# x and the query columns first, decode keys, values and S5 inputs in a later unit: a hybrid decoder step on one core

## The reference, cut to what matters

```
hn = rmsnorm(x, ln1_g)                     # x: 1024 prompt rows + 8 decode rows, width 1024
q, k, v, u = split(hn @ w_in)              # four groups of 512 columns
q, k = rope_partial(q) / 8, rope_partial(k)
attn = subln(softmax(q1 k1) v - lam * softmax(q2 k2) v)     # 4 heads, two maps each
                                           # prompt: causal; decode: 64 cache pages + the new key
s5   = glu(gelu(scan of 32 complex diagonal states driven by u))
x = x + concat(attn, s5) @ w_out
x = x + hierarchical_moe(rmsnorm(x))       # 32 experts, two per token
y = rmsnorm(x)                             # outputs also: new k, v and S5 states
```

## Time and profile before

| | us |
|---|---|
| median of 3 runs | 1478.14 (1476.67 to 1494.74) |
| profiled execution | 1475.24 |
| its span | 1473.5 |
| TensorE busy | 1284.7 (87%) |
| VectorE busy | 522.2 (35%) |
| ScalarE busy | 248.1 (17%) |
| POOL busy | 212.9 (14%) |
| mean of DMA | 311 GB/s |

### The profile page before, as it was taken

The page is one execution under the profiler, slowest core; times in us unless marked ns, Lnnn a source line. Parts: engine busy times, 40 slices in busy tenths (PEclk is TensorE's granted clock), DMA queues, the critical chain, the costliest instruction groups (busy, mean ns, idle before and its releaser), DMA issues.

```text
span 1473.5 us, 26489 instructions
## 1 busy us (share of the span) xinstructions
PE 1284.7 (87%) x8952; PEld 670.8 (46%) x8952; DVE 522.2 (35%) x1430; ACT 248.1 (17%) x473; POOL 212.9 (14%) x327
## 2 busy tenths in 40 slices
PE   4799899999889878899869999987799999999930
PEld 2455565654334335566654443433344444444410
DVE  1461344443564555455531121134221121112126
ACT  2200111120122222233321000000111111111111
POOL 1101204040401100000010000000112222222121
PEclk9899999999988989999999999986999999999975
DMA  9499979979987987999996998998899999999754
GB/s 355 173 318 317 340 258 304 344 236 319 313 286 250 366 285 251 368 330 312 325 372 253 337 337 294 314 348 309 284 332 363 368 372 360 367 364 373 259 202 186
DMA packets 186454, 458.35 MB, mean 311 GB/s; under 512 B 24177, under 2 KB 24561, under 8 KB 177778
## 3 DMA queue, kind: packets, MB, share of 16 engines
q1 hardware_dynamic: 165906, 394.41, 75.6%
q0 software_dynamic: 20448, 62.59, 12.7%
HBM read 421.92 MB, written 33.80 MB: 309 GB/s over the span
## 4 chain that ended last, share of the span: by engine, by line
PE 71%; DMA 9%; DVE 8%; SPq 5%; issue 3%; DVEq 2%; ACT 1%; POOL 1%; ACTq 0%; POOLq 0%; PEldq 0%
PE WA L1764 53%; PE SC L1764 7%; PE OD L1764 6%; DMA ring<-in_cacheK 3%; SPq L489 3%; DMA ring<-in_cacheV 2%; PE WA L2110 2%; DMA arena<-in_x_s 1%; SPq L477 1%; PE WA L1865 1%; DVE arena L1733 1%; DVE st L1105 1%; DMA ring<-h_scratch,idc 1%; DMA xm<-in_xT 1%; DVE arena L1746 1%
## 5 line engine op out<-in xcount | busy, mean ns | idle before, releaser
L1764 PE MATMUL WA<-arena 128*128 128x512 f32 (+9 forms) x1440 | 351.8, 428 | 15.3 <-issue 7.1
L1764 PE MATMUL WA<-arena,xm 128*128 128x512 f32 (+2 forms) x768 | 315.7, 619 | 8.7 <-DMA arena<-in_w_out 6.6
L1764 PEld LDWEIGHTS WA<-arena 128*128 128x128 f32 (+2 forms) x1440 | 192.6, 195 | 148.6 <-issue 132.6
L1764 PEld LDWEIGHTS WA<-arena,xm 128*128 128x128 f32 (+1 forms) x768 | 123.5, 182 | 164.1 <-issue 155.9
L1764 PE MATMUL WA<-xm,arena 128*128 128x512 f32 x192 | 88.8, 610 | 1.7 <-ACT arena L936 1.3
L553 POOL TENSOR_TENSOR st<-st,consts 128x1 f32<-128x1 f32 (+2 forms) x18 | 13.8, 765 | 465.5 <-DVEq L1139 279.0
L1764 PE MATMUL OD<-ring,sall 128*32 128x512 f32 x512 | 69.8, 660 | 11.9 <-DMA ring<-in_cacheV 11.9
L1764 PE MATMUL OD<-ring,qpad 128*32 128x128 f32 x2048 | 64.1, 275 | 8.9 <-DMA ring<-in_cacheK 8.7
L1764 PE MATMUL SC<-ring,qpad 128*32 128x128 f32 x2048 | 64.4, 276 | 7.7 <-DMA ring<-in_cacheK 7.5
L1676 DVE TENSOR_TENSOR xm<-WA,colw 128x960 f32<-128x960 f32 x16 | 18.5, 1158 | 147.1 <-PE WA L2110 147.1
L1676 DVE TENSOR_TENSOR arena<-WA,colw 128x960 f32<-128x960 f32 x16 | 18.5, 1158 | 137.5 <-PE WA L2110 137.3
(11 more groups left out here) (359 smaller groups left out, 1250.0 us busy)
## 6 DMA issues: line engine op xcount, KB each, us to landing
ring<-in_cacheK SPq DMA_DIRECT2D x512, 256.0 KB, 4.7
ring<-in_cacheV SPq DMA_DIRECT2D x512, 256.0 KB, 4.7
arena<-in_w_gu SPq DMA_DIRECT2D x16, 2048.0 KB, 8.6
arena<-in_w_dn SPq DMA_DIRECT2D x16, 1024.0 KB, 12.5
ring<-in_w_gu SPq DMA_DIRECT2D x8, 2048.0 KB, 8.6
xm<-in_w_gu SPq DMA_DIRECT2D x8, 2048.0 KB, 8.6
arena<-in_w_in SPq DMA_DIRECT2D x32, 256.0 KB, 10.2
ring<-in_w_dn SPq DMA_DIRECT2D x8, 1024.0 KB, 12.6
```

Source lines behind the costliest of these rows:

```text
L1764: return pe.matmul(out, lhsT, rhs, start=first, stop=last, **kw)
```

## The change

The loads of SP are issued in another order: all of x, then `w_q`, then `w_u`, then the pages. `w_k` and `w_v` come in two loads of 2 MB from POOL's queue, once `qpad` is written. POOL issues only three loads ahead of the statistics; the other six follow the root. `dqkv` is replaced by `dq` (queries alone, four column groups of 128 columns, ahead of the 9 one-column products) and by `dkv` and `dk2` (keys, values and u), planned later; `dprep` is a planned unit, carried out by VectorE ahead of its first `u` evacuation. `qpad` is written by 8 copies. The planner begins with other values of its bank, page and pace counters. `lam` moves behind the queries.

```diff
@@ -59,7 +59,8 @@
     return {
-"stats": [(("ss",), 2)], "dqkv": [(("dp",), 1)], "dprep": [(("rep",), 2), (("dqt",), 1)],
+"stats": [(("ss",), 2)], "dq": [(("dp",), 1)], "dprep": [(("dqt",), 1), (("rep",), 2)],
+"dkv": [(("dkv",), 1)], "dk2": [(("dkt",), 1)],
 "u": [(("u",) + a[:2], 1)] if first else [],
@@ -79,12 +80,12 @@
-    dec = []
+    dec = [(("dprep",), 2.5, [(("dq",), 6.0)])]
     for x in range(NPASS):
...
         for y in range(SPP):
-            dec.append((("K", x, t, g, y), 1.95, [(("ov", SPP * x - 1), 0.8)] if x else []))
+            dec.append((("K", x, t, g, y), 1.95, [(("ov", SPP * x - 1), 0.8)] if x else [(("dprep",), 0.5)]))
 dec += [(("m1", x), 0.8, [(dec[-1][0], 0.9)]), (("m2", x), 0.3, [(("m1", x), 3.3)]),
@@ -106,6 +107,9 @@
     proj += [(("u", n, a, f), half, []) for f in range(2)]
+    if (n, a) == (3, 0):
+        proj.append((("dkv",), 7.5, [(("dprep",), 20.0)]))
+    proj.append((("dk2",), 0.9, [(("dkv",), 6.0)]))
     for i in range(NT):
@@ -136,9 +140,9 @@
-    s5 = [(("s5a",), 0.0, [])]
+    s5 = [(("s5a",), 0.0, [(("dprep",), 2.0)])]
     for n in range(NQ):
-x = [(("bY", n - 1, 1), 0)] if n else [(("u", 3, 1, 1), 4.0), (("s5a",), 60.0)]
+x = [(("bY", n - 1, 1), 0)] if n else [(("u", 3, 1, 1), 4.0), (("dk2",), 3.0), (("s5a",), 60.0)]
@@ -178,9 +182,9 @@
     at = {k: 0 for k in lists}
-    end, free, nxt = {}, [0.0] * BANKS, 0
-    plan, t = [("stats",), ("dqkv",), ("dprep",)], 0.0
-    land, gone, due = [0.0, 0.0], [], 0.0
+    end, free, nxt = {("dq",): 0.0}, [0.0] * BANKS, 3
+    plan, t = [("stats",), ("dq",)], 0.0
+    land, gone, due = [4.0, 10.0], [], 4.0
     kept, never = {}, 1e9
@@ -258,6 +262,10 @@
+    first = PLAN.index(("u", 0, 0, 1))
+    DVE_PLAN = PLAN[:first] + [("dprep",)] + [u for u in PLAN[first:] if u != ("dprep",)]
+    assert PLAN.index(("dprep",)) > first
     POW = {}
...
@@ -473,8 +482,10 @@
         sp.dma_start(xm[:, k, :], io["xT"][k, :, :]).then_inc(s_xk[k], 16)
-        for n, w in enumerate((w_q, w_k, w_v, w_u)):
-            sp.dma_start(w[:, k, :], io["w_in"][n, k, :, :]).then_inc(s_wk[k], 16)
+    for k in range(KD):
+        sp.dma_start(w_q[:, k, :], io["w_in"][0, k, :, :]).then_inc(s_wq, 16)
+    for k in range(KD):
+        sp.dma_start(w_u[:, k, :], io["w_in"][3, k, :, :]).then_inc(s_wk[k], 16)
@@ -536,17 +547,16 @@
     gp.dma_start(rope[:, :, :], io["rope"]).then_inc(s_cst, 16)
-    gp.dma_start(br[:, :], io["b_r"].partition_broadcast(128)).then_inc(s_cst, 16)
-    gp.dma_start(wr[:, :, :], io["w_r"]).then_inc(s_cst, 16)
-    gp.dma_start(bglu[:, :], io["b_glu"]).then_inc(s_cst, 16)
-    gp.dma_start(lamv[:, :, :], io["lamv"].partition_broadcast(128)).then_inc(s_lamv, 16)
-    gp.dma_start(par, io["s5_par"]).then_inc(s_ld5, 16)
-    gp.dma_start(bc, io["s5_bc"]).then_inc(s_ld5, 16)
     def stats():
         gp.memset(qpad[:, :, :, :], 0.0).then_inc(s_qbd, 1)
-        gp.wait_ge(s_cst, 96)
+        gp.wait_ge(s_cst, 48)
         root(rstd[:, :], ("stats",))
+        gp.dma_start(lamv[:, :, :], io["lamv"].partition_broadcast(128)).then_inc(s_lamv, 16)
+        gp.dma_start(bglu[:, :], io["b_glu"]).then_inc(s_lamv, 16)
+        gp.dma_start(br[:, :], io["b_r"].partition_broadcast(128)).then_inc(s_lamv, 16)
+        gp.dma_start(wr[:, :, :], io["w_r"]).then_inc(s_lamv, 16)
+        gp.dma_start(par, io["s5_par"]).then_inc(s_ld5, 16)
+        gp.dma_start(bc, io["s5_bc"]).then_inc(s_ld5, 16)
@@ -559,17 +569,22 @@
-    def dqkv():
-        gp.wait_ge(s_drope, 1)
+    def dprep():
+        gp.wait_ge(s_qbd, 2)
+        for n, w in enumerate((w_k, w_v)):
+            gp.dma_start(w, io["w_in"][n + 1, :, :, :].rearrange("k p n -> p k n")).then_inc(s_wkv, 16)
+    def dkv():
+        gp.wait_ge(s_drope, 2)
         gp.dma_start(io["v_s"], dv[:, :]).then_inc(s_dst, 16)
...
-    def dprep():
-        gp.wait_ge(*filled("dqt"))
+    def dk2():
+        gp.wait_ge(*filled("dkt"))
         gp.memset(U[:, :, 0:NB], 0.0)
...
         gp.drain().then_inc(s_uz, 1)
-        gp.wait_ge(s_qbd, 2)
+        gp.wait_ge(s_qbd, 3)
...
@@ -732,10 +747,10 @@
-    def dqkv():
+    def dq():
         act.wait_ge(*filled("dp"))
-        for n, out in enumerate((qk[0:NB, 0:QKW], qk[0:NB, QKW:2 * QKW], dv[:, :], du)):
-            act.activation(out, slot("dp")[32 * n:32 * n + NB, 0:QKW], ACT.Copy)
+        for c in range(4):
+            act.activation(qk[0:NB, 128 * c:128 * c + 128], slot("dp")[32 * c:32 * c + NB, 0:128], ACT.Copy)
         act.drain().then_inc(free_sem("dp"), 1)
@@ -743,6 +758,15 @@
         act.drain().then_inc(free_sem("rep"), 1)
+        act.wait_ge(s_lam, 1)
+        act.activation(lamt[:, 2:4], lamt[:, 0:2], ACT.Exp).then_inc(s_lam, 1)
+    def dkv():
+        act.wait_ge(*filled("dkv"))
+        for n, out in enumerate((qk[0:NB, QKW:2 * QKW], dv[:, :], du)):
+            act.activation(out, slot("dkv")[32 * n:32 * n + NB, 0:QKW], ACT.Copy)
+        act.drain().then_inc(free_sem("dkv"), 1)
+        act.drain().then_inc(s_dq, 1)
@@ -752,7 +776,7 @@
         else:
-            act.wait_ge(*filled("dqt"))
+            act.wait_ge(*filled("dkt"))
             act.wait_ge(s_dst, 48)
@@ -916,9 +940,7 @@
-    act.wait_ge(s_lam, 1)
-    act.activation(lamt[:, 2:4], lamt[:, 0:2], ACT.Exp).then_inc(s_lam, 1)
...
@@ -1004,22 +1026,27 @@
     def lam():
-        dve.wait_ge(s_lamv, 16)
+        dve.wait_ge(s_lamv, 64)
         dve.tensor_tensor(lamv[:, 0, :], lamv[:, 0, :], lamv[:, 1, :], MUL)
...
         dve.drain().then_inc(s_lam, 1)
+    def lam_map():
         dve.wait_ge(s_lam, 2)
...
         dve.drain()
+        dve.scalar_tensor_tensor(wmap[:, 0:SPP, :].rearrange("p y h -> p (y h)"), consts[:, C_M1:C_M1 + SPP * H],
+                                 lamt[:, 7:8], consts[:, C_M0:C_M0 + SPP * H], MUL, ADD)
+        dve.drain()
...
     def stats():
-        lam()
-        dve.wait_ge(s_cst, 96)
+        dve.memset(rstd[:, NT:NT + 1], 1.0)
+        dve.wait_ge(s_cst, 48)
         for k in range(KD):
@@ -1028,46 +1055,55 @@
         dve.drain().then_inc(free_sem("ss"), 1)
-        dve.memset(rstd[:, NT:NT + 1], 1.0)
-        dve.scalar_tensor_tensor(wmap[:, 0:SPP, :].rearrange("p y h -> p (y h)"), consts[:, C_M1:C_M1 + SPP * H],
-                                 lamt[:, 7:8], consts[:, C_M0:C_M0 + SPP * H], MUL, ADD)
-        dve.drain()
         dve.wait_ge(s_col, 1)
...
         root(("stats",))
+        dve.drain().then_inc(s_rstd, 1)
+    def dq():
+        dve.wait_ge(s_dq, 1)
+        dve.tensor_scalar(qk[0:NB, 0:QKW], qk[0:NB, 0:QKW], rstd[0:NB, NT:NT + 1], None, MUL)
+        dve.drain()
+        rotate(qk[0:NB, 0:QKW], NB, NT)
+        dve.drain().then_inc(s_drope, 1)
+        for i in range(NT):
+            dve.tensor_scalar(diag[:, i, :], ident, rstd[:, i:i + 1], None, MUL)
+        dve.drain().then_inc(s_rep, 1)
+    def dprep():
+        dve.wait_ge(s_qbd, 1)
+        dve.wait_ge(*filled("dqt"))
+        src = slot("dqt")[:, 0:H * NB].rearrange("p (h x y) -> p h x y", h=H, y=SPP)
+        for h in range(H):
+            for c in range(2):
+                dve.tensor_copy(qpad[64 * c:64 * c + 64, h, :, :].rearrange("p (x y) n -> p x (y n)", y=SPP)
+                                [:, :, 2 * h + c::40], src[64 * c:64 * c + 64, h, :, :])
+        dve.drain().then_inc(free_sem("dqt"), 1)
+        dve.drain().then_inc(s_qbd, 1)
+        lam()
         dve.tensor_scalar(bglu[:, :], bglu[:, :], 0.5, None, MUL)
...
         dve.memset(st[:, :], 1.0)
...
-        dve.drain().then_inc(s_rstd, 1)
-        for i in range(NT):
-            dve.tensor_scalar(diag[:, i, :], ident, rstd[:, i:i + 1], None, MUL)
-        dve.drain().then_inc(s_rep, 1)
-    def dqkv():
-        dve.wait_ge(s_dq, 1)
+        dve.drain()
+    def dkv():
+        lam_map()
+        dve.wait_ge(s_dq, 2)
         r = rstd[0:NB, NT:NT + 1]
-        dve.tensor_scalar(qk[0:NB, :], qk[0:NB, :], r, None, MUL)
+        dve.tensor_scalar(qk[0:NB, QKW:2 * QKW], qk[0:NB, QKW:2 * QKW], r, None, MUL)
         dve.tensor_scalar(dv[:, :], dv[:, :], r, None, MUL)
...
         dve.drain()
-        rotate(qk[0:NB, :], NB, NT)
+        rotate(qk[0:NB, QKW:2 * QKW], NB, NT)
         dve.drain().then_inc(s_drope, 1)
...
-    def dprep():
-        dve.wait_ge(s_qbd, 1)
-        dve.wait_ge(*filled("dqt"))
-        src = slot("dqt")[:, 0:2 * H * NB].rearrange("p (a h b) -> p a h b", a=2, h=H)
-        for h in range(H):
-            for c in range(2):
-                for y in range(SPP):
-                    dve.tensor_copy(qpad[64 * c:64 * c + 64, h, y::SPP, 8 * y + 2 * h + c],
-                                    src[64 * c:64 * c + 64, 0, h, y::SPP])
-        dve.tensor_copy(knT[:, :, :], src[:, 1, :, :])
-        dve.tensor_copy(usT, slot("dqt")[:, 2 * H * NB:3 * H * NB].rearrange("p (n b) -> p n b", n=4))
-        dve.drain().then_inc(free_sem("dqt"), 1)
+    def dk2():
+        dve.wait_ge(*filled("dkt"))
+        dve.tensor_copy(knT[:, :, :], slot("dkt")[:, 0:H * NB].rearrange("p (h b) -> p h b", h=H))
```

(48 more changed lines are left out.)

13 lines of the change are left out of this document (7 added, 6 removed).

## The result

The changed kernel took 1464.5 us (median of 4 runs, 1460.34 to 1464.86), the kernel before 1479.36 beside it: ratio 0.9885, 95% interval 0.9851 to 0.9919. It is 15 to 17 us shorter, less than the 2% that count as a difference here. The forecast was 1461 within 1446 to 1475. The profiled execution took 1464.86, its span is 1463.1; before it was 1475.24 and 1473.5. The kernel before was profiled once only, so how far its own places move from one execution to the next is not known.

What follows compares the result with a forecast made beforehand. TensorE was taken as nearly always busy from 60.6 to 1050 us, the opening using neither TensorE nor DMA well. Gain 18.9 less 2 for page waits, 17 us: 1475.2 to 1458, plus 2.9 for a median, 1461 us, range 1446 to 1475.

Steps and rivals of the forecast that it cites:

- x first: Opening: TensorE's statistics start at about 8.5 instead of 14.7 us and end at 27.4, not 40.9.
- Queries alone: Opening, behind the statistics: query projection over at 29.3, root at 34.0, queries rotated at 36.3; u(0,0) from 31.4 to 40.2.
- Transposes, replication, first pages: Opening, behind u(0,0) ending at 40.2: transposes and replication end at 42.8, first page unit at about 46.2 instead of 66.2.
- Weights on POOL's queue: Key and value weights, asked for at about 43, land by 64; sharing with pages costs 2 us, at worst 6.
- rival 4: Weights come too late because VectorE's two-port modes keep GpSimd from writing DMA descriptors: 1490; chance 0.02.
- The sum: TensorE's work through u(0,0) and all decode projections done at 50.9 instead of 69.8: gain 18.9 us.
- Both stand in a stretch where TensorE is never idle, so both count in full: Later projection of keys, values and u inputs (7.1 us) and eight transposes (1.0 us) cost TensorE their full time.
- rival 2: Page stream, not TensorE, sets the end: gain 23.6 us, added 8.1 us fall into idle time, 1451; chance 0.14.
- A new order deals these anew; I allow 8 us either way: TensorE's waits from 400 to 760 us, 49 us idle, change with the planner's order: 8 us either way, no mean.
- 3: Attention stretch redrawn, heads back to back without page units, added 1.9 us waits: 1484, in full 1507; chance 0.06.
- 5: Opening: constants land at 12, not 8.5, holding the statistics' start; gain 3.5 us smaller, 1464; chance 0.02.
- 1: Contention: third and fourth page units wait the full 6 us, first key evacuation 5.6; gain 7, 1471; chance 0.14.

Runs made afterwards that it cites:

- e11: Changed kernel with half of each cache page left out of its transfer (zeros instead): 1432.16 us, ratio 0.9679.
- e4: Changed kernel with key and value weights loaded from SP's queue, behind the u weights and ahead of the first page, instead of POOL's queue: 1472.94 us, ratio 0.9949.
- e1: Kernel before with one edit, SP issuing all eight chunks of x ahead of the weight chunks: 1468.21 us, ratio 0.9933.
- e2: Kernel before with x first and six of POOL's loads moved behind the root, lam behind qpad; single projection and old order kept: 1468.49 us, ratio 0.9906.
- e5: Kernel before with only the planner's new start values, so 337 of 523 places in the order differ: 1499.02 us, ratio 1.0107.
- e3: Changed kernel with the order of units of the kernel before, behind a head written by hand: 1471.55 us, ratio 0.9929.
- e7: Changed kernel with its own order through dk2 and the order of the kernel before for every unit beyond: 1467.23 us, ratio 0.9884.
- e12: Changed kernel with seven of eight chunks of the projection dkv left out: 1464.17 us, ratio 0.9878.
- e9: Kernel before with half of each cache page left out of its transfer (zeros instead): 1456.75 us, ratio 0.9839.
- e10: Kernel before with only the planner's new start values and half of each cache page left out of its transfer: 1457.19 us, ratio 0.985.
- e8: Changed kernel without the split: u weights ahead of the others, u(0,0) right behind the statistics, then the single decode projection: 1475.01 us, ratio 0.9947.

## Why the prediction was right, step by step

**x first.** Start of the statistics 8.5, measured 8.55, released by the load of `rope` as worked out; end 27.4, measured 26.7. The half pace of the first chunk (3.78) was there.

**Queries alone.** The 64 records took 1.94 us for a predicted 1.95, over at 29.0 (29.3). Root at 33.2 (34.0), rotation over at 35.3 (36.3). The 1.7 us at half pace in `u(0,0)` weren't paid: 7.13 us. In e11, whose opening has the same instructions on TensorE, the same line took 8.83. It is a price that comes in some executions.

**Transposes, replication, first pages.** 40.2 for a predicted 42.8, and 43.70 for 46.2, the difference being the 1.7, the start 0.5 us earlier and transposes under the end of `u(0,0)`.

**Weights on POOL's queue.** Issued at 40.3 and 41.2, landed after 10.6 and 17.3 us, so by 58.5 (64 was predicted), far ahead of their use at 102.3. The page wait was 2.2 us, predicted 2. That the number came out hides two errors. The pages of the third unit were asked for from 45.0 on, not 48, and the split was not even in bytes: none of them moved until 48, and from 51 to 56 SP's queue moved 0.62 MB and POOL's 1.41 MB. The queues from 51 to 56 us (packets, MB, share of 16 engines):

```profile
q0 software_dynamic: 345, 1.41, 69.3%
q1 hardware_dynamic: 343, 0.62, 32.2%
```

Even were the packets, 345 and 343. The rule of the Trainium skill (DMA: Bandwidth & Descriptors, SWDGE vs HWDGE vs iDMA), that each DMA engine goes round between the queues, agrees with that; it is not an even split of the bytes, which the prediction made of it. e4 is the other case, weights and pages in one queue, with 5.0 us of waits. The trap of rival 4 (the Trainium skill, SBUF - State Buffer, "DVE blocks DMA") did not show: VectorE was busy for 8.46 of the ten microseconds up to 60, and the 4.2 MB came in 18 us. Whether any of its operations there ran in a two-port mode no run shows, so this does not test the trap.

**The sum.** 18.9 us on TensorE against 19.2 and 21.3 at the last `u`. The start moved ahead is shown term by term by the timeline and by e1 and e2. That the sum met its number so closely is partly luck: the opening gained 2.6 us more than predicted, the half pace behind the page wait cost 1.7 more, and the 7.1 us of added work were no full term (below).

**What failed** is behind the last `u`. "The distance to before should stay near this through 165, 400, 760 and 1050" was wrong: 9.4 to 16.8 were left at the last `v`. The prediction priced page waits for the third and fourth unit alone and gave the rest of the stretch none. From the last `u` to the last `v` TensorE's idle time went from 9.7 to 17.0 us (14.5 the second time), 3.6 (1.1) of it for pages and 1.6 (2.0) for `ddiag`, and its busy time from 220.3 to 222.8 (220.0); that is the loss of 9.8 (4.5). With half of each page left out the two orders take 219.7 and 220.1, so nearly all of it hangs on the DMA stream and not on other engines. That the *new order* makes pages late is shown for e5 only; e1, e2, e3 and e7 lost 3 to 6 there too with the old order behind the opening, so a new order is not needed for a part of it; what that part hangs on was not tried.

"A new order deals these anew; I allow 8 us either way": mis-sized. e5 alone is 23 us at the experts, 14.4 of them from the last `u` to the last `v`. The prediction looked at the waits from 400 to 760 alone; the same view from 60 to 400 has 8.2 us of page waits in the kernel before.

"Both stand in a stretch where TensorE is never idle, so both count in full": `dkv` took 7.2 us as predicted, but with 6.0 of them left out e12 was only 3.5 and 1.4 us sooner at the last `u`, no sooner at the experts (1021.3 against 1018.1 and 1015.7) and no shorter. This is what rival 2 said of the added work ("fall into idle time further down"). A busy TensorE at 60 to 165 was no evidence against it: the pages were just in time, and of the work taken away in e12 a good part turned into waits for them.

**Idle time from 400 to 760** is 53.5 us, within 38 to 60. Its content was dealt anew as expected: one wait of 11.1 for combined probabilities instead of eight of together 15.3, 6.5 for w_out, and 14.4 for pages (keys in `SC` 6.8, values 7.6), where before these two had 11.0 (6.5 and 4.5).

**Rivals.** 3 (slower by attention) did not happen here: the experts' start moved ahead by 14 to 16. 5 was in the sum, and the constants came at 8.55. Of 1, the third unit waited 2.2 and not 6, and the first key evacuation did wait for the stores, 4.4 us on ScalarE, of which TensorE saw 0.5; the prediction had costed this at nothing to 5.6. Of 2, the 23.6 us did not come (19.2 and 21.3 at the last `u`, 13.6 and 16.0 at the experts), but what it says of the added work did.

**Luck at the end.** The forecast had 17 us from the opening and none from the rest. Measured were 19 to 21, a loss of 5 to 10 and between +5.7 and -1.0 behind it. e4 has the same order of instructions on TensorE and 18.1 us at the last `u`, and had 1.0 left at the experts in its profile. That the end came out 3.5 us from 1461 owes something to chance.

**The experts** took 398.8 and 398.9 us in the two profiles of the changed kernel and 396.4 before. The change is not the reason: the fourteen profiles fall into 396.1 to 396.7 (before, e1, e3, e4, e9, e10, e12) and 398.2 to 400.3 (the changed kernel twice, e2, e5, e7, e8, e11), each with old and changed orders in it. What makes the difference stays open. So does why e4 and e8 are 6 to 13 us longer between `v` and the experts in the changed order of units.

## What to carry to other kernels

Where TensorE and a paced stream are both near full, TensorE's busy share alone doesn't say which of them is the bound: halve the bytes of the stream, and the time of the same instructions with that much less of it is there to read. Price a redealt order by all waits of the stretches behind it; here each additional microsecond of idle time cost 1.35 to 1.5. Take waits and stretch from the same window. And profile both kernels more than once before a difference of some microseconds in the middle is explained: here the same instructions were 7.4 us apart at one place. Work saved where the stream is just in time may bring little, as in e12.

## What the runs showed of the hardware

The pace of TensorE behind a wait of 1.5 to 1.6 us varies from execution to execution with the same instructions: half a unit and a `u` half took 1.76 and 4.66 us in one profile, 1.08 and 3.70 in the other. Behind the waits of 3.7 (e5), 4.2 (changed kernel) and 7.8 us (e3) shown above it was half pace. Of the 32 executions of the kernel before that ran beside e1 to e4, from 1470.7 to 1492.1 us, the longer ones had in the main the lower granted clock (0.944 in the shortest, 0.933 in the longest). DMA moved 403 GB/s between 20 and 30 us with transfers of SP's queue alone, and 388 between 50 and 60 with 2.07 MB from SP's queue and 1.81 MB from POOL's. From 51 to 56, with transfers under way in both, the two queues moved 343 and 345 packets but 0.62 and 1.41 MB (347 and 342 packets, 0.63 and 1.40 MB from 50 to 55 in the second profile).
